# Expert slots, norm pass and hand-over order in a fused two-block transformer kernel in float32

## The reference

```python
def hier_moe(h, ...):                 # first block, after its attention
    ...                               # router: group, then two experts; gates[token, expert]
    for e in range(N_EXPERTS):        # 32
        hid = jax.nn.silu(t @ w_eg[e]) * (t @ w_eu[e])     # 1024 -> 512
        out = out + gates[:, e:e + 1] * (hid @ w_ed[e])    # 512 -> 1024
# first_block ends with: return rmsnorm(x, normf_g)
for l in range(DEPTH_2):              # second_block, 2 layers
    x = x + 0.5 * rmsnorm_2(swiglu(rmsnorm_2(x, ffn1_pre_g[l]), w_ffn1_in[l], w_ffn1_out[l]), ffn1_post_g[l])
    h = rmsnorm_2(x, mix_pre_g[l])
    (z, xbc, dt_raw, rq, rk, rv, rg, aq, ak, av, gate) = jnp.split(h @ w_in[l], offsets, axis=-1)
    ...
    branch = jnp.einsum('blmc,mcd->blmd', ys, w_branch[l])
    gates = jax.nn.sigmoid((gate + b_gate[l]).reshape(bsz, L, N_BRANCH, D_MODEL))
    y = jnp.sum(gates * branch, axis=2) @ w_out[l]
    x = x + rmsnorm_2(y, mix_post_g[l])
    x = x + 0.5 * rmsnorm_2(swiglu(rmsnorm_2(x, ffn2_pre_g[l]), w_ffn2_in[l], w_ffn2_out[l]), ffn2_post_g[l])
```

## Time and profile before

| what | us |
|---|---|
| median of 3 runs | 2131.18 (2127.7 to 2131.92) |
| the profiled execution | 2128.98 |
| its span, first to last instruction | 2127.2 |
| PE busy in it | 1950.0 (92%) |
| DVE busy | 1150.1 (54%) |
| ACT busy | 884.1 (42%) |

### The profile page before, as it was taken

The page is one execution under the profiler, slowest core; times in us unless marked ns, Lnnn a source line. Parts: engine busy times, 40 slices in busy tenths (PEclk is TensorE's granted clock), DMA queues, the critical chain, the costliest instruction groups (busy, mean ns, idle before and its releaser), DMA issues.

```text
span 2127.2 us, 29966 instructions
## 1 busy us (share of the span) xinstructions
PE 1950.0 (92%) x12346; PEld 1546.6 (73%) x12346; DVE 1150.1 (54%) x1583; ACT 884.1 (42%) x1288; POOL 47.5 (2%) x99
## 2 busy tenths in 40 slices
PE   7988766777779999999999999999999999999998
PEld 7873121121148887899899888898878999998887
DVE  5751100110137657477865676476674779656763
ACT  5521000000025444457744554354444577445552
POOL 0010000000000000000000100000000000001000
PEclk9988778777789999999999999999999999999999
DMA  7568999999995554543445455454545434355552
GB/s 280 194 262 327 421 421 421 421 421 421 421 368 176 213 186 171 184 158 120 149 159 180 180 193 185 177 178 182 195 178 186 170 120 149 140 181 188 188 191 87
DMA packets 66900, 486.05 MB, mean 228 GB/s; under 512 B 7424, under 2 KB 7424, under 8 KB 8544
## 3 DMA queue, kind: packets, MB, share of 16 engines
q1 hardware_dynamic: 65632, 476.25, 59.1%
q0 software_dynamic: 1152, 8.16, 1.0%
HBM read 483.33 MB, written 1.05 MB: 228 GB/s over the span
## 4 chain that ended last, share of the span: by engine, by line
PE 76%; DMA 10%; SPq 7%; DVE 3%; ACT 2%; issue 2%; POOL 1%; DVEq 0%; ACTq 0%; POOLq 0%
PE bank L1540 22%; PE bank L1555 12%; PE bank L1640 11%; DMA work<-in_w_experts 10%; PE bank L1873 8%; PE bank L1553 7%; SPq L1440 6%; PE bank L1569 3%; PE bank L1551 2%; PE bank L1368 2%; PE bank L1398 1%; PE bank L1421 1%; PE bank L1091 1%; ACT work L2319 1%; PE bank L2058 1%
## 5 line engine op out<-in xcount | busy, mean ns | idle before, releaser
L1518 DVE TENSOR_TENSOR ring_parts<-ring,work_parts 128x2048 fp32r<-128x2048 f32 x188 | 430.2, 2291 | 237.3 <-ACT work_parts L1511 223.1
L1511 ACT ACTIVATE work_parts<-ring 128x2048 fp32r<-128x2048 f32 x168 | 321.0, 1913 | 217.6 <-PE bank L1640 80.0
L1540 PE MATMUL bank<-work_parts 128*128 128x256 f32 x1376 | 317.6, 283 | 1.2 <-DVE ring_parts L1518 1.2
L1540 PE MATMUL bank<-rows_parts,work_parts 128*128 128x256 f32 x864 | 245.1, 284 | 0.0
L1540 PE MATMUL bank<-rows_parts,ring_parts 128*128 128x256 f32 x864 | 244.4, 283 | 0.0
L1540 PEld LDWEIGHTS bank<-work_parts 128*128 128x128 f32 x1376 | 238.9, 192 | 1.7 <-issue 1.5
L1555 PE MATMUL bank<-work_parts 128*128 128x512 f32 x840 | 213.2, 393 | 0.0
L1553 PEld LDWEIGHTS bank<-work_parts,ring_parts 128*128 128x128 f32 x1280 | 174.6, 190 | 12.3
L1398 PE MATMUL bank<-work 128*32 128x512 f32 x640 | 126.3, 886 | 59.2 <-DMA work<-in_w_experts 59.2
L1553 PE MATMUL bank<-work_parts,ring_parts 128*128 128x256 f32 x1280 | 178.5, 282 | 0.0
L1555 PEld LDWEIGHTS bank<-work_parts 128*128 128x128 f32 x840 | 150.1, 189 | 26.2
(11 more groups left out here) (387 smaller groups left out, 3150.7 us busy)
## 6 DMA issues: line engine op xcount, KB each, us to landing
ring<-in_w_layers SPq DMA_DIRECT2D x242, 1024.0 KB, 4.9
work<-in_w_experts SPq DMA_DIRECT2D x136, 1024.0 KB, 26.8
ring<-in_w_experts SPq DMA_DIRECT2D x48, 1024.0 KB, 26.7
ring<-in_w_first SPq DMA_DIRECT2D x16, 1024.0 KB, 5.5
columns<-in_w_experts SPq DMA_DIRECT2D x8, 1024.0 KB, 26.6
work<-in_post POOLq DMA_DIRECT2D x3, 1024.0 KB, 5.0
...
```

What stands on the lines that cost most here:

```text
L1511: act.activation(his[j % len(his)], m.ring[U.slot(names[j])], ACT.Copy).then_inc(F["unit_hi"], 1)
L1518: dve.tensor_tensor(m.ring_r[slot], m.ring[slot], his[j % len(his)].bitcast(F32), ALU.subtract).then_inc(F["unit_lo"], 1)
L1540: mm = pe.matmul(out, w, x, start=k + n == 0, stop=k == KT - 1 and n == 2)
```

## The change

Places for experts go from 18 to 19, and the ones used twice are places 3 to 7 instead of 6 to 11. The first `gather_columns` stand ahead of the gate copies. `keep_clock` puts matmuls of ones, whose result nobody reads, around the router's rank product (13 and 3) and after the last turn (8). The down product runs column half by column half, and its first half is copied and added back while the second is multiplied; the host orders the down units to match. In the norm after the experts, x times gain is squared beside x, and POOL works the second root out of both sums. In the bridges DVE normalises token half 0 before it weights (0, 1), and takes the columns before it weights (1, 1); the second `turn_half` comes later on PE. mx.out runs token half by token half. The mixer's low columns are made by two instructions of 128 columns from PSUM, and dt becomes a split product. g.1.0 and g.1.1 stand inside `attend`. `LAYER_JOBS` gets seven empty places, so that it has 232. The mixer's end may run one unit further ahead, with other homes for high parts.

```diff
+SKIPPED = range(4, 18, 2)
+def with_skips(jobs):
+    return [n for job in jobs for n in ([None, job] if job in [f"f1.in.{i}.a" for i in SKIPPED] else [job])]
+LAYER_JOBS = ([f"f1.n.{i}" for i in range(4)] + with_skips(ffn_in_jobs("f1"))
               + [f"f1.out.{n}.{t}" for n in range(2) for t in range(2)]
               + [f"mx.n.{i}" for i in range(4)]
...
              + [f"mx.out.{n}.{i}" for n in range(2) for i in range(2)])
+END_HOME = [(6, None, 4, 5)[j % 4] for j in range(14)] + [4, 3, 5, 6, None, 4]
+END_READ = (["b.0.1", "b.0.2", "ap.1.1.1.1", "ap.1.1.1.1"] + END_SPLIT[:10]
+            + ["g.2.2", "g.2.3", "g.2.3", "b.2.0", "b.2.1", "b.2.2"])
...
+def keep_clock(pe, m, bank, n):
+    for _ in range(n):
+        pe.matmul(bank[:, 0:T], m.c["ones"][:, 0:P], m.c["ones"], start=True, stop=True)
 def route_tensor(pe, m, ps, B, F):
+    keep_clock(pe, m, ps[B.bank("n2.2")], 13)
     pe.wait_ge(*F.at("chosen"))
     B.claim(pe, "rank")
...
...
-    moe_select(dve, m, m.sel, 0).then_inc(sel_ready, 1)
+    moe_select(dve, m, m.sel, 0).then_inc(M["sel"], 1)
...
+    for g in range(2):
+        dve.wait_ge(M["gathered"], g + 1)
+        gather_columns(dve, m, ps, g).then_inc(M["columns"], 1)
...
-EXPERT_SLOTS = 18
+EXPERT_SLOTS = 19
+SHARED_FROM = 3
...
-    return u if u < EXPERT_SLOTS else u - 12
+    return u if u < EXPERT_SLOTS else u - EXPERT_SLOTS + SHARED_FROM
+def shared(u):
+    return SHARED_FROM <= slot_of(u) < SHARED_FROM + LOADS - EXPERT_SLOTS
...
-    for g in range(2):
-        dve.wait_ge(M["gathered"], g + 1)
-        gather_columns(dve, m, ps, g).then_inc(M["columns"], 1)
...
-        act.wait_ge(M["used"], (i + 1) * LOADS + LOADS)
         for n in range(2):
+            act.wait_ge(M["used"], (i + 1) * LOADS + DOWN_UNIT + 4 * (n + 1))
...
-        for f in range(4):
-            for n in range(2):
-                w = unit(i, DOWN_UNIT + f * 2 + n)
+        def sums(n):
+            pe.wait_ge(M["rows"], since(i * 2 + n + 1))
+            for t in range(TT):
+                if n == 1:
+                    pe.wait_ge(M["added"], added_since(i * 4 + t + 1))
+                pe.matmul(ps[(SUM, TURN)[t]][:], m.selgT[:, t * P:(t + 1) * P], m.ym[:, n * 512:(n + 1) * 512],
+                          start=True, stop=True).then_inc(M["summed"], 1)
+        for n in range(2):
+            for f in range(4):
+                w = unit(i, DOWN_UNIT + n * 4 + f)
                 for e in range(QUAD):
                     mm = pe.matmul(ps[DOWN + n][rows_of(e), :], m.hidT[:, f * P + e * CAP:f * P + (e + 1) * CAP],
                                    w[:, e, :], start=f == 0, stop=f == 3)
                 mm.then_inc(M["used"], 1)
-        pe.wait_ge(M["rows"], since(i * 2 + 2))
-        for q in range(4):
-            t, n = q // 2, q % 2
-            if q >= 2:
-                pe.wait_ge(M["added"], added_since(i * 4 + q - 1))
-            pe.matmul(ps[(SUM, TURN)[q % 2]][:], m.selgT[:, t * P:(t + 1) * P], m.ym[:, n * 512:(n + 1) * 512],
-                      start=True, stop=True).then_inc(M["summed"], 1)
+                if (n, f) == (1, 1):
+                    sums(0)
+        sums(1)
...
     for unit in OUT_SPLIT:
         load_after(unit)
+        if unit == "out.1.0":
+            load(18, 0)
     sp.wait_ge(*B.filled("route"))
     load(17, 0)
...
-def whole_half(pe, B, U, ps, m, job, unit, t, ready=None):
+def whole_half(pe, B, U, ps, m, job, unit, t, ready=None, between=None):
...
     for c in range(2):
+        if between and c == 1:
+            between()
...
-    turn_half(pe, B, ps, m, F, f, 1)
     B.claim(pe, jobs[1])
-    whole_half(pe, B, U, ps, m, jobs[1], units[1], 0)
+    whole_half(pe, B, U, ps, m, jobs[1], units[1], 0, None, lambda: turn_half(pe, B, ps, m, F, f, 1))
...
-OUT_ORDER = {"f1": ((0, 0), (1, 0), (0, 1), (1, 1)), "mx": ((0, 0), (0, 1), (1, 0), (1, 1)),
-             "f2": ((0, 0), (1, 0), (0, 1), (1, 1))}
+OUT_ORDER = ((0, 0), (1, 0), (0, 1), (1, 1))
...
-    for n, t in OUT_ORDER[f]:
+    for n, t in OUT_ORDER:
         job = f"{f}.out.{n}.{t}"
         c = slice(n * 512, (n + 1) * 512)
-        if (n, t) == (1, 1):
+        if (n, t) == (0, 1):
             scaled(0)
+        elif (n, t) == (1, 1) and next_columns:
+            next_columns(0)
...
-    if next_columns:
-        next_columns(0)
     scaled(1)
...
+            if between and k == KT // 2 - 1:
+                between()
...
+    def out_rows(held, ready):
+        for t in range(TT):
+            for n in range(2):
+                B.claim(pe, f"mx.out.{n}.{t}")
+        parts = {}
+        for u in range(2):
+            for n in range(2):
+                parts[n, u] = unit_parts(pe, m, U, F, "end", END_SPLIT, 16 + 2 * n + u, m.ehi_r, KT // 2)
+                part_rows(f"mx.out.{n}.0", parts[n, u], u, 0, held, ready if n == 0 else None)
+        for n in range(2):
+            part_rows(f"mx.out.{n}.1", parts[n, 0], 0, 1, held).then_inc(U.parts_sem, 1)
+            part_rows(f"mx.out.{n}.1", parts[n, 1], 1, 1, held)
...
+    pe.wait_ge(*F.at("wdt_lo"))
+    wdt = [w.rearrange("p (k n) -> p k n", k=KT) for w in m.wdt_r]
     for k in range(KT):
-        mm = pe.matmul(ps[B.bank("dt")][0:16, 0:T], wdt[:, k, :], m.hT[:, k, :], start=k == 0, stop=k == KT - 1)
+        for n, (w, x) in enumerate(passes_of([w[:, k, :] for w in wdt], [x[:, k] for x in moving])):
+            mm = pe.matmul(split(ps[B.bank("dt")][0:16, 0:T], TT), w, x, start=k + n == 0, stop=k == KT - 1 and n == 2)
...
-        for n, (name, held) in enumerate((("g", moving), ("b", (m.yhi_r[b - 1], m.ylo_r[b - 1])))):
-            if n == 1:
-                pe.wait_ge(*F.at("end_lo", b))
-            for i in range(4):
-                job = f"{name}.{b}.{i}"
-                B.claim(pe, job)
-                parts = unit_parts(pe, m, U, F, "end", END_SPLIT, (b - 1) * 8 + n * 4 + i, m.ehi_r, KT)
-                split_columns(pe, B, ps, job, parts, held)
+        for i in range(2 if b == 1 else 0, 4):
+            end_columns("g", b, i, moving)
+        pe.wait_ge(*F.at("end_lo", b))
+        for i in range(4):
+            end_columns("b", b, i, (m.yhi_r[b - 1], m.ylo_r[b - 1]))
...
         dve.wait_ge(*F.at("mx.hi", 4 * t + i + 1))
-        whole = dve.tensor_tensor(m.hT[:, c, tokens], half_of(ps, B, job, t), bc(m.lp["gmix"][:, c], [P, 2, P]), ALU.mult)
-        if t == 0:
-            step(whole)
-        else:
-            whole.then_inc(B.free(job), 1)
-            dve.wait_ge(*B.drained(job))
-        dve.tensor_tensor(m.mhlo_r[:, t, c, :], m.hT[:, c, tokens], m.mh_r[:, t, c, :].bitcast(F32),
-                          ALU.subtract).then_inc(F["mx.cols"], 1)
+        bank = half_of(ps, B, job, t)
+        for k in range(2):
+            kk = 2 * i + k
+            ins = dve.scalar_tensor_tensor(out=m.mhlo_r[:, t, kk, :], in0=bank[:, k, :], scalar=m.lp["gmix"][:, kk:kk + 1],
+                                           in1=m.mh_r[:, t, kk, :].bitcast(F32), op0=ALU.mult, op1=ALU.subtract)
+        ins.then_inc(F["mx.cols"] if t == 0 else B.free(job), 1)
...
+                root, mean = m.ss[:, t:t + 1], m.pr[:, t:t + 1]
                 pool.wait_ge(*first_layer.at("f2.pss", t + 1))
                 root_of_mean_of(pool, first, m, m.ss, t, first_layer["f2.prstd"])
-            for t in range(TT):
+                pool.wait_ge(*first_layer.at("f2.prstd", t + 1))
                 pool.wait_ge(*first_layer.at("f2.ss", t + 1))
-                root_of_mean_of(pool, first, m, m.ss, t, first_layer["f2.rstd"])
+                for _ in range(2):
+                    first(pool.tensor_tensor(mean, mean, root, ALU.mult))
+                root_of_mean_of(pool, first, m, m.pr, t, first_layer["f2.rstd"])
...
-                act.wait_ge(M["added"], turns * 4 + 2 * t + 1)
-                act.activation(m.xn[:, t, :], m.x[:, t, :], ACT.Square, scale=D ** -0.5,
+                act.wait_ge(M["added"], turns * 4 + 2 + t)
+                act.activation(m.spare[t], m.x[:, t, :], ACT.Square, scale=D ** -0.5,
                                accum_out=m.ss[:, t:t + 1]).then_inc(first_layer["f2.pss"], 1)
-            for t in range(TT):
-                act.wait_ge(*first_layer.at("f2.x", t + 1))
-                act.activation(m.xn[:, t, :], m.x[:, t, :], ACT.Square, scale=D ** -0.5,
-                               accum_out=m.ss[:, t:t + 1]).then_inc(first_layer["f2.ss"], 1)
+                act.wait_ge(*first_layer.at("f2.pss", t + 1))
+                act.wait_ge(gained, t + 1)
+                act.activation(m.spare[t], m.xn[:, t, :], ACT.Square, scale=D ** -0.5,
+                               accum_out=m.pr[:, t:t + 1]).then_inc(first_layer["f2.ss"], 1)
...
+            for t in range(TT):
+                dve.wait_ge(M["added"], turns * 4 + 2 + t)
+                dve.tensor_tensor(m.xn[:, t, :], m.x[:, t, :], m.normf, ALU.mult).then_inc(gained, 1)
...
+                dve.wait_ge(gained, t + 1)
```

(8 more changed lines are left out.)

134 lines of the change are left out of this document (77 added, 57 removed).

## The result

The changed kernel takes 2099.57 us in the median of 4 runs (2098.51 to 2100.93), the kernel before in the same session 2130.93. The ratio is 0.9853, with a 95% interval from 0.9839 to 0.9868. The forecast was 2105 with a range from 2098 to 2114: right in sign and range, 5.4 us too high. The profiled execution has a span of 2096.7 against 2127.2, so the traces differ by 30.5 where the working gave 26.1.

A forecast was written before the change was run, and what follows sets the result against it. The prediction took PE to bound the kernel up to the experts, the weight stream through them, and PE again in the layers. Its terms summed to -26.1 us, span 2101.1, hence 2105 us, with 8 in 10 runs from 2098 to 2114.

The forecast's parts named there:

- A: Start of the experts: ones at the rank product, earlier gate products, earlier first reload, one load fewer; -9.1 us.
- B: Norm behind the experts: copy of one half, two matmuls instead of four, rearranged squares and roots; -2.2 us.
- D: Bridge from mixer to f2: token half 1's norm hides behind products, about 2.5 us less idle per layer; -5.0 us.
- E: Bridge from f2 to the next f1: 232 jobs avoid a shared bank, so two PE waits shrink; -1.8 us.
- F: Attend in the mixer: products g.1.0 and g.1.1 fill PE's waits there; -1.7 us.
- R2: Rival: the weight stream runs dry once, in the first turn, where the margin is 0.9 us; 2108 us, chance 0.04.
- R4: Rival: places 3 to 7 starve the weight stream in every turn, making the kernel slower; 2135 us, chance 0.02.
- C: Bridge from f1 to mixer: earlier low columns, later norm of token half 1; -1.0 us first layer, 0 second.
- G: The mixer's dt as a split product: -0.6 us in each layer, -1.2 us in all.
- Clock: Slow-clock losses removed by shorter gaps: -3.0 us at two bridges, -1.2 us behind the experts, -4.2 us together.
- R1: Rival: the clock does not follow; losses vanish at some bridges, appear at others; 2113 us, chance 0.12.
- R3: Rival: token half 1 is late at the bridges, so 5 us of the gains come back; 2110 us, chance 0.12.

The follow-up runs named there:

- raise_early: The changed kernel with DVE's counters for turn 0 raised right behind its scaled columns, ahead of the gate copies: 2101.36 us.
- before_router_ones: The kernel before with the sixteen matmuls of ones at the router added and nothing else: 2129.30 us.
- columns_last: The changed kernel with DVE's low columns put back behind the last weighting and the update of x: 2112.76 us.
- jobs_225_columns_last: The kernel of columns_last with 225 jobs instead of 232: 2113.89 us.
- out_by_columns: The changed kernel with mx.out column half by column half and the old order of the bridge from mixer to f2: 2109.01 us.
- no_tail_ones: The changed kernel without the eight matmuls of ones behind the experts: 2100.10 us.

## Why the prediction was right, point by point

A, B and the sum of D and E with its clock make 20.4 of the 30.5 us in the traces and agree with the forecast within 0.7. One link of A failed, and D and E were put down in part to the wrong pieces of the change. The rest was forecast at 5.0 and is 10.1: F was too small, and some 3 of it are luck, the clock as it happened to stand in two single profiles.

**A, -9.1.** Measured -7.8 (3.3, 2.6 and 1.9 in the read of the last unit). Right in each link but one. Ones, clock, three reads, one load: 5.86 for 5.8, 3.84 for 3.57, 2.57 for 2.6, 2.7 for 2.49. The step that failed is "with it none", the sentence that DVE's columns ahead of the gate copies leave nothing to wait for. The edit also put DVE's counters behind the copies, and that took the 0.6 that raise_early gave back. I had counted the instructions that were moved and not the one that they were moved past. The 1.2 that the old order was said to give back is larger too: before_router_ones takes 1.5 longer than raise_early from gather to gate, and loses 1.7 more by the clock behind that wait. A second loss of 0.8 is the late last read. Rival R2 did not occur, and R4 is refuted.

**B, -2.2.** From the last unit's start 12.84 became 10.0, so -2.8; the two squares beside each other cost nothing, where I had put +0.3.

**C, -1.0.** The exchange of waits is as described. But the 2.05 that the first layer gained is clock. The kernel before with ones at the router has the same code at this bridge and takes 69.64 there, not 72.14; its PE row shows the full clock where that of the kernel before, first below, shows the slow one:

```profile
816.13 0.77 PE L1873 MATMUL bank<-work_parts,rows_parts 128*128 128x512 f32 x1 [2.06 <-DVE work_parts L2410]
819.76 0.47 PE L1880 MATMUL bank<-work_parts,rows_parts 128*128 128x512 f32 x1 [2.07 <-DVE work_parts L2417]
```

Against that, C is worth -0.3 from the earlier transposes and +0.4 behind them: nothing, in both layers, as long as the clock holds. What it changes, by these profiles, is how often the clock holds. With the low columns behind the last weighting (the kernel before, before_router_ones, columns_last, jobs_225_columns_last) this stretch took 69.6 to 69.9 us at four bridges and 71.5 to 72.7 at the other four; with the order of the change it took 70.1 at all twenty bridges of ten profiles. So the forecast's -1.0 is a fair mean, and that the traces show twice as much is the luck of one slow bridge. DVE's row for the eight small instructions, which stand ahead of the norm of half 1 and are part of why it is late, has 2.16 us:

```profile
1540.30 2.16 DVE L2473 SCALAR_TENSOR_TENSOR work_parts<-bank,work,rows_parts 128x128 fp32r<-128x128 f32 x8 [0.59 <-ACT rows_parts L2208]
```

The estimate from the figure of the Trainium skill ("VectorE: DVE Perf Modes", the section on the TRN2 errata) was 2.1 us; here the trace agrees.

**D and E, -6.8 and clock -3.0.** With its share of the clock D measured -6.7 and E -3.2, where -6.6 and -3.2 were forecast. E had one wait wrong by name: the 0.9 beside the 1.59 was not for L1805 but for the columns of L1788, the third of its waits in the earlier trace rows. The idle time there went from 2.52 to 0.65, so 1.9 for the 1.8 of the forecast. The 3.0 of clock are those of one profile of the kernel before: in before_router_ones, with the same code there, the three first halves take 5.14, 3.81 and 3.81 us, so only 1.3 was lost. The size was right and a part of the cause wrong: I gave D to the order of mx.out and E to the banks. out_by_columns shows the size (8.3 for both layers when all of that bridge is undone); columns_last shows that the order of mx.out gives nothing without the columns ahead of the last weighting (9.6 lost at the same bridges), and jobs_225_columns_last that the bank count gives nothing without them either.

**F, -1.7, and G, -1.2.** G is 0.8 in each layer instead of 0.6 (3.56 became 2.74: 0.114 a pass where I took 0.124). F is the term of the sum that was mis-sized: -3.6. I counted only the wait for L2390. Beside it went 0.6 of the eight products behind the wait and about 0.4 of a wait for a low part. Of the 4.4 us by which the sum was too small, F and G are 2.4, C (clock, as said) 1.2 and the clock at the first bridge 1.3, less 0.7 at A and B. The last 1.0 of the 5.4 is that the median lies 2.9 above the profiled span, not 4.0.

**Clock, -4.2.** -2.5 instead of -1.2 at the first bridge in this profile, but in seven of the nine profiles of kernels with eight ones the gain is 0.9 to 1.1. So the 2.5 are luck of the profiled run. The forecast's half was about right in size and wrong in its reason: no_tail_ones gains 1.4 without any ones. R1 did not come true: in all nine profiles that keep the changed bridges, those into f2 take 16.2 to 16.6, with no idle time in them. With a wait of 1.9 or more it fell at all eight FFN bridges of columns_last, out_by_columns and jobs_225_columns_last; with the old bridges it held at one of three in the kernel before and at two of three in before_router_ones. The Trainium skill's sentence ("TensorE: Matmul & The Clock Gate", Part 1: The HAM clock gate) that the moment is not tied to the program agrees with this, and with the two bridges into f2 of the kernel before: the same code takes 19.78 us in one layer and 18.15 in the other.

R3 did not show: no second transposes wait at D or E.
